# Interleaving sixteen heads of attention with projection and output units in a two-block transformer kernel

## What is computed

```python
def mla_mixer(x, positions, cos, sin, w_in, q_norm, kv_norm, w_uq, w_uk, w_uv, w_o):
    h = x @ w_in
    c_q, c_kv, k_r = jnp.split(h, [512, 768], axis=-1)      # then rms_norm of c_q and c_kv
    q = (c_q @ w_uq).reshape(B, S, 16, 128 + 64)            # 128 plain + 64 rotated by position
    q_rope, k_rope = apply_rope(q[..., 128:], ...), apply_rope(k_r, ...)
    k_nope = (c_kv @ w_uk).reshape(B, S, 16, 128)
    v = (c_kv @ w_uv).reshape(B, S, 16, 128)
    for blk in range(2):                                    # 128 queries each, keys up to their end
        s = (q_nope @ k_nope + q_rope @ k_rope) * scale, masked
        outs.append(softmax(s) @ v)
    return concatenate(outs).reshape(B, S, 2048) @ w_o
```

## Time and profile before

| | |
|---|---|
| median of 3 runs | 1832.79 us (1831.98 to 1833.97) |
| the profiled execution, its own time | 1833.46 us |
| its span, first to last instruction | 1831.3 us |
| PE / PEld busy | 98% / 95% of the span |
| DVE / ACT / POOL busy | 62% / 53% / 6% |
| HBM read | 294.57 MB, 161 GB/s over the span |
| granted TensorE clock, mean | 0.997 of full |
| first block's attention with output units | 37.18 to 199.98 us |
| layer norm behind it, to the first matmul of `up0` | 199.98 to 206.28 us |

### The profile page before, as it was taken

How to read it: one execution, slowest core, us unless ns; L and a number is a source line. 1 busy time by engine, 2 the same in 40 slices (tenths; PEclk the granted TensorE clock), 3 DMA queues, 4 the chain that set the end, 5 groups by cost and what they waited for, 6 DMA issues and landing times.

```text
span 1831.3 us, 33012 instructions
## 1 busy us (share of the span) xinstructions
PE 1787.0 (98%) x14206; PEld 1741.0 (95%) x14206; DVE 1133.6 (62%) x1826; ACT 971.6 (53%) x1531; POOL 115.7 (6%) x120
## 2 busy tenths in 40 slices
PE   8889999999999999999999999999999999999998
PEld 8778999998889999999999999999999999999998
DVE  6656798666468885655556765554555555765554
ACT  6555576556357664654444445443554443765443
POOL 0001000010010001100011020001100002020002
PEclk9999999999999999999999999999999999999999
DMA  6333455545334555455554535555454555235552
GB/s 213 102 115 104 163 189 185 184 150 182 130 135 161 186 187 190 165 171 173 173 176 149 175 134 174 175 177 176 150 166 158 188 185 173 93 138 186 186 187 98
DMA packets 85040, 297.74 MB, mean 163 GB/s; under 512 B 10496, under 2 KB 13440, under 8 KB 84896
## 3 DMA queue, kind: packets, MB, share of 16 engines
q1 hardware_dynamic: 82400, 294.16, 48.3%
q10 hardware_dynamic: 2496, 1.49, 0.3%
HBM read 294.57 MB, written 1.05 MB: 161 GB/s over the span
## 4 chain that ended last, share of the span: by engine, by line
PE 89%; DVE 6%; ACT 2%; POOL 1%; issue 1%; DMA 1%; ACTq 0%; DVEq 0%; SPq 0%; POOLq 0%
PE ps L1361 28%; PE ps L1363 28%; PE ps L1362 28%; PE ps L1408 1%; POOL acc L809 1%; DVE w_lo L833 1%; DMA raw<-stream 1%; ACT w_hi L385 1%; DVE y L869 1%; PE ps L1562 0%; PE ps L1727 0%; DVE y L881 0%; PE ps L1736 0%; ACT a_hi L427 0%; DVE tmp L912 0%
## 5 line engine op out<-in xcount | busy, mean ns | idle before, releaser
L833 DVE TENSOR_TENSOR w_lo<-raw,w_hi 128x1024 fp32r<-128x1024 f32 x557 | 692.9, 1253 | 391.6 <-ACT w_hi L385 264.9
L385 ACT ACTIVATE w_hi<-raw 128x1024 fp32r<-128x1024 f32 x557 | 579.8, 1050 | 183.0 <-DMA raw<-stream 159.7
L1361 PE MATMUL ps<-a_hi,w_hi 128*128 128x256 f32 (+1 forms) x2336 | 667.2, 286 | 8.5 <-DVE a_lo L896 3.6
L1363 PE MATMUL ps<-a_hi,w_lo 128*128 128x256 f32 (+1 forms) x2336 | 662.8, 284 | 0.0
L1362 PE MATMUL ps<-a_lo,w_hi 128*128 128x256 f32 (+1 forms) x2336 | 662.4, 284 | 0.0
L1361 PEld LDWEIGHTS ps<-a_hi,w_hi 128*128 128x128 f32 x2336 | 441.6, 189 | 15.3 <-issue 8.0
L1363 PEld LDWEIGHTS ps<-a_hi,w_lo 128*128 128x128 f32 x2336 | 442.1, 189 | 0.0
L1362 PEld LDWEIGHTS ps<-a_lo,w_hi 128*128 128x128 f32 x2336 | 440.1, 188 | 0.2
L1361 PE MATMUL ps<-h_hi,w_hi 128*128 128x256 f32 (+1 forms) x1376 | 389.8, 283 | 4.3 <-ACT work L674 2.7
L1363 PE MATMUL ps<-h_hi,w_lo 128*128 128x256 f32 (+1 forms) x1376 | 389.2, 283 | 0.0
L1362 PE MATMUL ps<-h_lo,w_hi 128*128 128x256 f32 (+1 forms) x1376 | 388.7, 282 | 0.0
(11 more groups left out here) (228 smaller groups left out, 1476.0 us busy)
## 6 DMA issues: line engine op xcount, KB each, us to landing
raw<-stream SPq DMA_DIRECT2D x557, 512.0 KB, 3.3
x<-xT SPq DMA_DIRECT2D x1, 1024.0 KB, 6.9
out<-x SPq DMA_DIRECT2D x8, 128.0 KB, 1.7
work<-pT ACTq DMA_DIRECT2D x2, 256.0 KB, 2.7
par<-params ACTq DMA_DIRECT2D x1, 283.5 KB, 4.5
tmp<-causal ACTq DMA_DIRECT2D x1, 208.0 KB, 2.5
con<-consts ACTq DMA_DIRECT2D x1, 194.5 KB, 6.2
tmp<-pos ACTq DMA_DIRECT2D x1, 128.0 KB, 14.9
```

The costliest lines, as they stand in the source:

```text
L385: nc.scalar.activation(w_hi[:, u % SLOTS, :], raw[:, u % SLOTS, :], ACT.Copy).then_inc(w_hi_ready, 1)
L833: nc.vector.tensor_tensor(w_lo[:, u % SLOTS, :], raw[:, u % SLOTS, :], w_hi[:, u % SLOTS, :].bitcast(F32), ALU.subtract).then_inc(w_lo_rea ...
L1361: nc.tensor.matmul(dst, wh, xh, start=first, stop=False, skip_group_check=True)
L1363: return nc.tensor.matmul(dst, wl, xh, start=False, stop=last, skip_group_check=True)
```

## The change

1. **Attention.** The 16 heads run in one chain. The weights' order changes: rotated queries first, then plain ones, keys and values of the first half (10 units); then `mla_mid`, the second half's 10 units; then the 16 output units split by input half, 8 `mla_oa` (heads 0 to 7) and 8 `mla_ob` (heads 8 to 15). The chain has 18 steps. Step i is, on PE: scores of head i + 2, one unit of `mla_mid` or `mla_oa`, transposes of head i, product with values of head i - 1. Each `mla_oa` result is added to the residual by DVE (`part_ready`), and `mla_ob`'s is added to that. Transposes always use bank 6 and value products bank 7, where two banks each were used in turn.
2. **Decay rows.** `neg_c` is zeroed over all 128 partitions (one more DVE memset, before `kv_k`) and `spread_c` uses 128 rows of the identity and of `neg_c`.
3. **Gate tail.** ACT: `head_std(1)` stands before `gate_r(4)`, and `gate_r(7)` before `gla_high(3)`. DVE: `head_norm(1)` stands before the next `lo_next`.

```diff
-PHASES = [("mla_in", 7)]
-for _half in (0, 1):
-    PHASES += [(f"mla_qn{_half}", 4), (f"mla_qr{_half}", 2), (f"mla_kn{_half}", 2), (f"mla_v{_half}", 2)]
-PHASES += [("mla_o", 16), ("up0", 44), ("down0", 22), ("proj0", 2), ("gate0", 8),
+PHASES = [("mla_in", 7), ("mla_qr", 2), ("mla_qn", 4), ("mla_kn", 2), ("mla_v", 2), ("mla_mid", 10), ("mla_oa", 8), ("mla_ob", 8)]
+MLA_MID = (("qr", 0), ("qr", 1), ("kn", 0), ("qn", 0), ("qn", 1), ("v", 0), ("kn", 1), ("qn", 2), ("qn", 3), ("v", 1))
+MLA_MID_BANK = ((1,), (2,), (0, 1), (2,), (0,), (1, 2), (0, 1), (2,), (3,), (0, 1))
+MLA_O_BANK = (2, 3, 0, 1)
...
@@ ACT
+            for i in range(18):
+                u = BASE["mla_mid"] + i
+                if i + 1 < 16:
+                    exponentials(i + 1, 128, 256, sm_m)
+                hi_next(u)
+                if i < 10:
...
+                        mla_value(u, n, banks)
+                if i < 16:
+                    act.wait_ge(turned, i + 1)
+                    if i >= 2:
+                        act.wait_ge(mixed, i - 1)
+                    nc.scalar.activation(pt_m[:, i % 2, :], ps[:, 6, 0:384], ACT.Copy).then_inc(turned_sb, 1)
+                if 1 <= i <= 16:
+                    act.wait_ge(mixed, i)
+                    nc.scalar.activation(h_hi[:, i - 1, TOK], ps[:, 7, 0:SEQ], ACT.Copy).then_inc(h_hi_ready, 1)
...
             for n in range(6):
+                if n == 4:
+                    head_std(1)
                 gate_r(n)
...
                 if n == 4:
-                    head_std(1)
...
             gate_r(6)
-            for t in range(3, 6):
-                gla_high(t)
             gate_r(7)
-            for t in range(6, 8):
+            gla_high(3)
+            for t in range(4, 8):
                 gla_high(t)
@@ DVE
+            for i in range(18):
+                if i == 2:
+                    rope(1, 0, 3)
+                if i == 6:
+                    rope(1, 1, 3)
+                if i + 1 < 16:
+                    normalized(i + 1, 128, 256, sm_m)
+                lo_next(BASE["mla_mid"] + i)
+                if i >= 10:
+                    n = i - 10
+                    dve.wait_ge(unit_done, BASE["mla_oa"] + n + 1)
+                    nc.vector.scalar_tensor_tensor(y[:, n, TOK], x[:, n, TOK], ALPHA, ps[:, MLA_O_BANK[n % 4], 0:SEQ],
+                                                   ALU.mult, ALU.add).then_inc(part_ready, 1)
+                if i + 2 < 16:
+                    masked(i + 2, 0, 128, 256, sm_m, mask_m, True)
+                if 1 <= i <= 16:
+                    mixed_low(i - 1, H_SPLIT["mla"] + i, i - 1, 7)
...
             head_var(1)
+            head_norm(1)
             lo_next(u + 4)
-            head_norm(1)
             lo_next(u + 5)
...
             nc.vector.memset(v_sh[:, 0, :], 0.0).then_inc(v_zeroed, 1)
+            nc.vector.memset(neg_c, 0.0).then_inc(v_zeroed, 1)
@@ PE
-                nc.tensor.matmul(ps[:, 4 + t % 4, 0:T], ident[0:8, t:t + 1].to_broadcast([8, P]), neg_c[0:8, :],
+                nc.tensor.matmul(ps[:, 4 + t % 4, 0:T], ident[:, t:t + 1].to_broadcast([P, P]), neg_c,
                                  start=True, stop=True, skip_group_check=True).then_inc(q_spread, 1)
...
+            def mla_turn(t):
+                pe.wait_ge(probs, t + 1)
+                if t > 0:
+                    pe.wait_ge(turned_sb, t)
...
+            def mla_mix(t):
+                pe.wait_ge(turned_sb, t + 1)
+                if t > 0:
+                    pe.wait_ge(h_split, H_SPLIT["mla"] + t)
...
+            for i in range(18):
+                u = BASE["mla_mid"] + i
...
+                if i + 2 < 16:
+                    mla_scores(i + 2)
...
+                elif i == 6:
+                    pe.wait_ge(q_copied, 6)
+                    pe.wait_ge(v_copied, 5)
+                    mla_key(u, (0, 1))
...
+                    mla_out(u, 0, MLA_O_BANK[n % 4])
+
+                if i < 16:
+                    mla_turn(i)
...
+                if 1 <= i <= 16:
+                    mla_mix(i - 1)
+
             pe.wait_ge(h_split, H_SPLIT["ffn0"])
...
+            for n in range(8):
+                if n < 4:
+                    pe.wait_ge(part_ready, n + 5)
+                else:
+                    pe.wait_ge(y_ready, KD * LN["mla"] + n - 3)
+                mla_out(BASE["mla_ob"] + n, 1, MLA_O_BANK[n % 4])
```

More of the change, by code:

```diff
@@ L437, in exponentials @@
                                          accum_out=cols[:, at + 2 + b:at + 3 + b]).then_inc(exped, 1)
[L439 to L453, removed]
             def ffn(f):
@@ L590, in _ @@
             hi_next(u + 6)
[L592 to L618, removed]
@@ L922, in masked @@
                                         negate=True).then_inc(maxed, 1)
[L924 to L931, removed]
-                        mixed_low(first + t - 3, h_base + t - 2, h_tile + t - 3, (first + t - 3) % 2)
             def normalized(a, w0, w1, sm):
@@ new lines, in _ @@
+            for i in range(2):
+                lo_next(BASE["mla_qr"] + i)
+            lo_next(BASE["mla_qn"])
+            dve.wait_ge(kr_ready, 2)
+            rope(0, 0, 4)
+            lo_next(BASE["mla_qn"] + 1)
+            rope(0, 1, 5)
+            for i in range(2, 4):
+                lo_next(BASE["mla_qn"] + i)
+            for i in range(2):
+                lo_next(BASE["mla_kn"] + i)
+            lo_next(BASE["mla_v"])
+            masked(0, 0, 128, 256, sm_m, mask_m, True)
+            masked(1, 0, 128, 256, sm_m, mask_m, True)
@@ L1669, in _, with mla_query @@
-            each_unit("mla_o", mla_o)
+            def mla_query(u, bank, fresh=False):
+                pe.wait_ge(w_lo_ready, u + 1)
+                for q in range(2):
+                    for k in range(4):
+                        if fresh and q == 0:
+                            pe.wait_ge(c_split, k + 1)
+                        ins = three(ps[:, bank, q * SEQ:(q + 1) * SEQ], *tile(u, 4 * q + k),
+                                    b_hi[:, k, TOK], b_lo[:, k, TOK], k == 0, k == 3)
+                ins.then_inc(unit_done, 1)
@@ new lines, in mla_swap, with mla_key @@
+            def mla_swap(half, i, bank):
+                pe.wait_ge(qr_copied, 2 * half + i + 1)
+                nc.tensor.matmul(ps[:, bank, :], swap, qr_raw[:, 2 * i:2 * i + 2, :].rearrange("p a b -> p (a b)"),
+                                 start=True, stop=True).then_inc(qr_swapped, 1)
+            def mla_key(u, banks):
+                pe.wait_ge(w_lo_ready, u + 1)
+                for q in range(4):
+                    for k in range(2):
+                        ins = three(ps[:, banks[q // 2], (q % 2) * SEQ:(q % 2 + 1) * SEQ], *tile(u, 2 * q + k),
+                                    b_hi[:, 4 + k, TOK], b_lo[:, 4 + k, TOK], k == 0, k == 1)
+                ins.then_inc(unit_done, 1)
@@ new lines, in mla_value @@
+            def mla_value(u, banks):
+                pe.wait_ge(w_lo_ready, u + 1)
+                for m in range(2):
+                    tokens = slice(META + m * P, META + (m + 1) * P)
+                    for k in range(2):
+                        w = slice(512 * k, 512 * k + 512)
+                        ins = three(ps[:, banks[m], :], b_hi[:, 4 + k, tokens], b_lo[:, 4 + k, tokens],
+                                    w_hi[:, u % SLOTS, w], w_lo[:, u % SLOTS, w], k == 0, k == 1)
+                ins.then_inc(unit_done, 1)
@@ new lines, in mla_out @@
+            def mla_out(u, part, bank):
+                pe.wait_ge(w_lo_ready, u + 1)
+                for k in range(KD):
+                    ins = three(ps[:, bank, 0:SEQ], *tile(u, k), h_hi[:, KD * part + k, TOK], h_lo[:, KD * part + k, TOK],
+                                k == 0, k == KD - 1)
+                ins.then_inc(unit_done, 1)
+            u = BASE["mla_qr"]
+            mla_query(u, u % BANKS, True)
+            mla_query(u + 1, (u + 1) % BANKS)
+            u = BASE["mla_qn"]
```

304 lines of the change are left out of this document (181 added, 123 removed).

## The result

The changed kernel takes 1806.35 us (median of 4 runs, 1806.07 to 1806.87) where the kernel before, run beside it, takes 1832.39. The ratio is 0.9854, with a 95% interval from 0.9842 to 0.9866. Its profiled execution took 1806.16 us with a span of 1804.3 us; before these were 1833.46 and 1831.3. The predicted 1807.5 us is 1.2 us too slow.

What follows compares the result with a forecast made beforehand. PE bounds the program but idles in the first block's attention, waiting for DVE's divided probabilities. 18.9 + 3.3 + 3.1 = 25.3 us off 1833.46 gives 1808.2, median 0.67 lower: 1807.5 us, range 1804 to 1813.

Steps and rivals of the forecast that it cites:

- the divided probabilities: First block's attention: PE's transposes wait for DVE's divided probabilities, 14 times, 12.7 us.
- The count of PE's work: First block: 143.9 us of PE work in 162.80, so 18.9 us idle, all removed by the chain.
- The opening's 1.0: Start of the first block: the first unit waits k-tile by k-tile for normalised inputs, 1.0 us, between 0.7 and 1.7.
- The circle: Attention chain: DVE's and ACT's work from mask to next mask closes 0.3 us inside PE's step of 5.16 us.
- Rival 1: Attention chain: DVE and ACT end the step, PE waits 0.3 to 0.6 us in some 14 steps, +4 to +8; chance 0.15.
- Rival 2: Attention chain: prepared weights fall behind, units and heads no longer overlap, +45 us, 1852; from a 6.7 us step; chance 0.03.
- The sums of the layer norm: Layer norm behind the first block: no added PE wait for POOL's sums, 0 us, bounds 0 and +1.2.
- The gate tail: Gate tail: PE's waits of 1.04 and 2.67 us shrink, gla_o starts at 526.2 instead of 529.45, -3.3 us.
- the low end: Gate tail: only the first of PE's two waits goes, -1.0 us.
- Rival 4: Gate tail: only the first wait comes back, as gla_o then waits for w_lo or h_lo: -1.0, 1809.8 us; chance 0.10.
- Decay rows: Decay rows: with 128 rows four starts span 0.70 us instead of 1.09, eight times, -3.1 us, ends 0 and -3.9.
- Rival 3: Decay rows: the row count does not matter, PE shows 1.09 us again, time 1810.6 us; chance 0.06.

Runs made afterwards that it cites:

- e8: The changed kernel with the eight output units of the first half behind the chain instead of in its steps 10 to 17: 1814.88 us in one run.
- e10: The changed kernel with DVE making each mask of the first block's attention three times: 1811.29 us in one run.
- e9: The changed kernel with DVE making each mask of the first block's attention twice: 1804.27 us in one run.
- e7: The kernel before with only the second heads' square root and division earlier in the gate tail, gate 7 where it was: 1837.93 us in one run.
- e2: The kernel before with only the decay rows spread by 128-row matmuls: ratio 0.9987 of the kernel before.
- e5: The changed kernel with each decay row spread by 64 rows instead of 128: the four starts around it span 1.09 us.
- e6: The changed kernel with each decay row spread by 96 rows instead of 128: the four starts around it span 0.70 us.
- e11: The changed kernel with, in the last attention's steps 3 to 5, ACT's w_hi behind copies and h_hi, DVE's w_lo behind h_lo: 0.9864 of the kernel before.
- e12: The changed kernel with only ACT's w_hi moved behind copies and h_hi in the last attention, DVE's list unchanged: 1809.78 us in one run.

## Why the prediction was right

**What bounds the block.** Right that PE idled, and not for its own work; e8 shows the filling by taking it away. But the divided probabilities, which the prediction names as the cause, are half of it. The 12.7 us of the earlier trace rows are on the track of the weight loads. On PE's own track, over the same stretch, the view of waits has:

```profile
PE ps L1562 <- DVE tmp L939: 7.2, 7, 1.4
PE ps L1630 <- ACT work L610: 2.5, 2, 1.3
PE ps L1630 <- ACT work L615: 2.3, 2, 1.2
PE ps L1361 <- DVE h_lo L944: 1.9, 2, 0.9
```

So 4.8 us were waits of scores for ACT's copies of keys and values, and 1.9 us waits at the end of each half for h_lo. The prediction has these only in passing, as places where the new order leaves no wait. The chain removed all three; how much of the 19.84 us each is worth no run separates.

**The count of PE's work.** Right, and 0.9 us too high. A step is 3.03 for unit and the first matmul's hold (95.86 - 92.83), 0.33 for transposes, 0.65 for products and 1.13 for scores, in all 5.14, and 5.12 to 5.13 in most steps, where I had 5.16. A swap costs 0.85, not 0.9. With 0.04 a step that is 16 x 0.04 + 4 x 0.05 = 0.8 of the 0.9. The opening's 1.0 holds: the first three units take 9.64 us, 1.1 more than 3 x 2.84.

**The circle.** The direction is right, the number cautious: 0.7 us to spare in the step shown (bracket of 0.69 at the mask), not 0.3; w_lo ends 5.03 us after the unit where I had 5.4. "PE wants each result more than 5 us after it is made" is wrong for one result that I had not followed: h_lo has 3.3 us. It did no harm, since the circle closes, but it set the point at which e10 began to wait.

**Rival 1** didn't happen. It was priced with a bound of 0.3 us a step that is paid at once. 0.6 us more DVE work a step costs nothing (e9), and 1.2 us costs 7.4 us and not 13 (e10). **Rival 2**, units and heads that no longer overlap, wasn't reached; at a circle of 5.85 us PE's step is simply 5.85. What happens from 6.7 us on wasn't tried.

**The sums of the layer norm.** Right, 0: POOL's last sum is done at 177.6 us, PE wants it at 180.26.

**The gate tail.** -3.3 against -3.23. The step by step account held: the first wait gone, w_lo of gla_o's fourth unit done at 505.84 and gla_o at 505.95. Only the low end rested on a wrong idea, that a wait which is removed gives its own length (e7: 0.00). Rival 4 shared it.

**Decay rows.** -3.1 against 8 x 0.39 = -3.1. Rival 3, that the row count doesn't matter, is excluded by e2, and e5 and e6 show where it begins to matter.

**Elsewhere** I had forecast 0, and about 1 us was gained, which is the rest of the 2.0 by which the profiled execution beat the sum (27.3 against 25.3). Of it 0.3 is the wait for POOL's sums behind gla_o: its first matmul now has 0.21 where the earlier trace rows had 0.49. The 0.55 us between up0 and the gate tail lies at the layer norm behind the first ffn, and is a wait for POOL as well. The weight loads of its sums, before and after:

```profile
396.88 0.52 PEld L1408 LDWEIGHTS ps<-ones,acc 128*128 128x128 f32 x4 [0.25 <-POOL acc L809]
397.57 0.52 PEld L1408 LDWEIGHTS ps<-ones,acc 128*128 128x128 f32 x4 [0.17 <-POOL acc L809]
```

```profile
376.87 0.97 PEld L1477 LDWEIGHTS ps<-ones,acc 128*128 128x128 f32 x8
```

On PE these eight sums start 0.32 us behind the last product before and 0.11 after, and take 1.24 us to the next start before and 0.89 after, together 0.56 us. All five kernels without the chain have these two waits, all nine with it have none. So the prediction's zero for the sums held behind the attention and not here; why POOL is in time here once the chain stands in front is open.

**The median.** 1807.5 came out nearer than the sum did. The gain of the profiled execution was 2.0 us above the sum, the median only 1.2 below the forecast: I had taken off 0.67 us because the profiled execution before stood above its median, and the changed kernel's stands 0.19 below. That part of the agreement is luck.

## What to carry to other kernels

Count PE's own work start to start, per unit, scores, transposes and products; what the stretch has over that count is what filling can bring, and here the count was right to 1%. Fill a wait with whole units of other work, and ask first whether the circle of the other engines is shorter than the filled step: if it is, work added to it can cost nothing (e9), and results made ahead, here by 3.3 us or more, cover single delays; if it isn't, moving instructions around in the circle brought nothing in the one place where it was tried (e11, e12). And before a wait is counted as a gain, follow the chain that sets the next start: a wait beside it can go and the time stays the same (e7).

## What the runs showed of the hardware

A float32 matmul of 8 or of 64 rows between 128-row ones costs PE 0.39 us more than one of 96 or 128 rows, once for each visit, and its weight load is not longer (184 ns with 64 rows, 188 with 128). The granted clock of TensorE fell from 2.4 to 1.2 GHz behind a stretch in which PE was busy for 1.47 of 3.00 us, and was 0.52 over the next 10 us although the output units had begun; in the kernel before, where PE idled about an eighth of each half of the attention, it stayed at 2.4 GHz.
